# Two feature norms of a decoder step: sums of squares with tokens on partitions, deviation on three columns, result spread by TensorE

## What is computed

```python
def layer_norm(x, g=None, b=None):
    xf = x.astype(jnp.float32)
    mu = jnp.mean(xf, axis=-1, keepdims=True)
    var = jnp.mean(jnp.square(xf - mu), axis=-1, keepdims=True)
    y = (xf - mu) * lax.rsqrt(var + LN_EPS)
    if g is not None:
        y = y * g + b
    return y

def trunk_layer(x, c, pos, lw, st, mla_past):
    mod = jax.nn.silu(c) @ lw['w_ada'] + lw['b_ada']
    sh1, sc1, g1, sh2, sc2, g2 = jnp.split(mod[:, None, :], 6, axis=-1)
    u = x * (1.0 + sc1) + sh1
    mix, new_st = mixer_branches(u, pos, lw, st, mla_past)
    x = layer_norm(DEEPNORM_ALPHA * x + g1 * mix, lw['ln1_g'], lw['ln1_b'])
    u2 = x * (1.0 + sc2) + sh2
    f = (jax.nn.silu(u2 @ lw['w1']) * (u2 @ lw['w3'])) @ lw['w2']
    x = layer_norm(DEEPNORM_ALPHA * x + g2 * f, lw['ln2_g'], lw['ln2_b'])
    return x, new_st
```

## Time and profile before

| | |
|---|---|
| median of 3 runs | 1848.11 us (1847.59 to 1851.08) |
| the profiled execution | 1859.16 us, its span 1857.5 us |
| PE busy | 1707.7 us, 92% of the span |
| weight loads (PEld, beside PE) | 1476.6 us, 79% |
| DVE, ACT, POOL busy | 817.4, 738.3, 705.9 us |
| mean granted PE clock | 0.96 |

### The profile page before, as it was taken

How to read it: one execution, slowest core, us unless ns; L and a number is a source line. 1 busy time by engine, 2 the same in 40 slices (tenths; PEclk the granted TensorE clock), 3 DMA queues, 4 the chain that set the end, 5 groups by cost and what they waited for, 6 DMA issues and landing times. The chain is left out here.

```text
span 1857.5 us, 30323 instructions
## 1 busy us (share of the span) xinstructions
PE 1707.7 (92%) x10994; PEld 1476.6 (79%) x10994; DVE 817.4 (44%) x1881; ACT 738.3 (40%) x1112; POOL 705.9 (38%) x446
## 2 busy tenths in 40 slices
PE   3899999999999979999839999999999999899997
PEld 1788789987668869999718878898866677799996
DVE  0545367656431353332314642766654313533233
ACT  1444644333434344442224555342335342544332
POOL 0534456645123423333114444566361144233331
PEclk8899999999999989999969999999999999899999
DMA  9265424428575343444072653353475843444430
GB/s 355 90 222 189 143 93 158 159 91 278 183 282 178 134 181 141 155 151 145 23 294 91 238 201 102 109 186 133 127 270 178 283 172 126 173 142 153 155 141 29
DMA packets 73247, 309.10 MB, mean 166 GB/s; under 512 B 15555, under 2 KB 25091, under 8 KB 43011
## 3 DMA queue, kind: packets, MB, share of 16 engines
q1 hardware_dynamic: 73090, 307.09, 46.4%
HBM read 291.81 MB, written 15.25 MB: 165 GB/s over the span
## 5 line engine op out<-in xcount | busy, mean ns | idle before, releaser
L2052 POOL TENSOR_TENSOR wlx<-ring,wh 128x1024 fp32r<-128x1024 f32 x172 | 409.5, 2381 | 692.3 <-ACT wh L1069 686.2
L440 PE MATMUL zps<-uhi,wh 128*128 128x320 f32 x1232 | 386.4, 326 | 1.9 <-DVE qabs L1538 1.7
L441 PE MATMUL zps<-ulo,wh 128*128 128x320 f32 x1232 | 371.9, 314 | 0.0
L1069 ACT ACTIVATE wh<-ring 128x1024 fp32r<-128x1024 f32 x172 | 182.2, 1060 | 366.1 <-PE zps L441 229.9
L2157 POOL TENSOR_TENSOR wlo<-ring,whi 128x1024 fp32r<-128x1024 f32 x66 | 160.3, 2429 | 310.6 <-ACT whi L1069 310.3
L440 PEld LDWEIGHTS zps<-uhi,wh 128*128 128x128 f32 x1232 | 237.9, 193 | 15.8 <-issue 7.7
L441 PEld LDWEIGHTS zps<-ulo,wh 128*128 128x128 f32 x1232 | 238.2, 193 | 1.2 <-issue 0.4
L913 PE MATMUL zps<-xhi,whi 128*128 128x320 f32 x688 | 213.8, 311 | 0.0
L914 PE MATMUL zps<-xlo,whi 128*128 128x320 f32 x688 | 213.3, 310 | 0.0
L915 PE MATMUL zps<-xhi,wlo 128*128 128x320 f32 x688 | 213.2, 310 | 0.0
L445 PE MATMUL zps<-uhi,wlx 128*128 128x320 f32 x1232 | 207.8, 311 | 0.0
(11 more groups left out here) (285 smaller groups left out, 2570.6 us busy)
## 6 DMA issues: line engine op xcount, KB each, us to landing
ring<-wpack_dram SPq DMA_DIRECT2D x222, 1024.0 KB, 4.9
arena<-cache_dram SPq DMA_DIRECT2D x128, 320.0 KB, 4.8
arena<-stateA_dram SPq DMA_DIRECT2D x2, 2064.0 KB, 9.5
o_cn_s<-arena SPq DMA_DIRECT2D x2, 2064.0 KB, 11.2
arena<-stateD_dram SPq DMA_DIRECT2D x2, 2048.0 KB, 11.6
o_ret_s<-arena SPq DMA_DIRECT2D x2, 2048.0 KB, 11.0
x<-o_y SPq DMA_DIRECT2D x2, 1280.0 KB, 7.5
o_y<-x SPq DMA_DIRECT2D x4, 640.0 KB, 3.0
```

The lines of the kernel that those rows point to most:

```text
L440: nc.tensor.matmul(o, hi[:, k * P:(k + 1) * P], xh[:, k, :], start=k == 0, stop=False)
L441: last = nc.tensor.matmul(o, hi[:, k * P:(k + 1) * P], xl[:, k, :], start=False, stop=False)
L1069: return nc.scalar.activation(out, in_, func, **kw).then_inc(*ev(sem, label))
L2052: G().tensor_tensor(wlx[:, n % RING, half], ring[:, n % RING, half], wh[:, i, :], ALU.subtract).then_inc(*ev("pool_l", (q, i)))
```

## The change

It alters how the two norms get from the squares to the reciprocal deviation; the mean, the centring, the squares and the scaling stay.

- Sums of squares: the squares become the stationary operand, 128 tokens at a time (tokens 0 to 127, 128 to 255, 192 to 319), and one column of ones the moving one. That is three matmuls for each of the 8 feature blocks, each with one column of output. The sums lie in three columns, with tokens on partitions.
- The square root and the reciprocal work on these three columns, in `stats[:, 16:19]`, in place of 320 columns.
- A new step brings the reciprocals back to all partitions: for each group of tokens PE takes the column, broadcast to 128 columns, as stationary operand and columns of the identity as moving one, which writes the token's value in every partition. The result lies in a bank of its own, named `rstd`, which DVE's scaling reads. PE waits for the reciprocal before it, and DVE for PE after it.
- In norm 1 block 22 with its transposes stays between the sums of squares and the new step; block 23 comes after the new step.

```diff
@@ -261,6 +261,7 @@
         stats = sb("stats", [P, 128])
+        rsd = stats[:, 16:19]
@@ -879,13 +880,21 @@
-                        ps = bank("m", ("var", which), ("dve_r", ("xn", which, KC - 1)))
+                        ps = bank("m", ("var", which), ("act_n", ("std", which)))
                         for k in range(KC):
                             pe.wait_ge(*at("act_n", ("sq", which, k)))
-                            last = nc.tensor.matmul(ps[:, 0:T], ones, acc[:, k, :], start=k == 0, stop=k == KC - 1)
+                            for t, t0 in enumerate((0, P, T - P)):
+                                last = nc.tensor.matmul(ps[:, t:t + 1], acc[:, k, t0:t0 + P], ones[:, 0:1], start=k == 0 and t == 0, stop=k == KC - 1 and t == 2)
                         last.then_inc(*ev("pe_m", ("var", which)))
                         if which == 1:
-                            ada(22, 24, through=False)
+                            ada(22, 23, through=False)
+                        pe.wait_ge(*at("dve_r", ("rs", which)))
+                        ps = bank("m", ("rstd", which), ("dve_r", ("xn", which, KC - 1)))
+                        for t, (t0, tn) in enumerate(TOK):
+                            last = nc.tensor.matmul(ps[:, t0:t0 + tn], rsd[:, t:t + 1].to_broadcast([P, P]), ident[:, P - tn:P], start=True, stop=True)
+                        last.then_inc(*ev("pe_m", ("rstd", which)))
+                        if which == 1:
+                            ada(23, 24, through=False)
@@ -1389,7 +1398,7 @@
-                        go("act_n", ("std", which), std[:], m(("var", which))[:, 0:T], ACT.Sqrt, bias=cs("eps")[:, 0:1], scale=1.0 / D_MODEL)
+                        go("act_n", ("std", which), rsd, m(("var", which))[:, 0:3], ACT.Sqrt, bias=cs("eps")[:, 0:1], scale=1.0 / D_MODEL)
@@ -1978,9 +1987,8 @@
                         dve.wait_ge(*at("act_n", ("std", which)))
-                        V().reciprocal(banks["var", which][:, 0:T], std[:]).then_inc(*ev("dve_r", ("rs", which)))
-                        dve.wait_ge(*at("dve_r", ("rs", which)))
-                        return banks["var", which][:, 0:T]
+                        V().reciprocal(rsd, rsd).then_inc(*ev("dve_r", ("rs", which)))
+                        return m(("rstd", which))[:, 0:T]
```

## The result

The changed kernel takes 1866.3 us (median of 4 runs, 1862.8 to 1875.39) for 1848.11 before: ratio 1.0103, 95% interval 1.0064 to 1.0142, so it is slower by 12 to 26 us. The forecast was 1865.3.

A forecast was written before the change was run, and what follows sets the result against it. TensorE, busy 92%, bounds the kernel, with nothing hidden in the norms' serial chain. At the lower clock +3.3 us in each norm 2 and +5.3 in each norm 1 sum to +17.2 on 1848.11: 1865.3, range 1850 to 1871.

The forecast's parts named there:

- The sweep at full clock: Sums of squares on PE in each norm: 48 passes at 0.116 us plus tail, 5.64 us, +1.10 a norm.
- lower bound of 0.05 us a pass: Sums of squares: least time of a pass, read from 16 loads of 32 columns in 0.80 us.
- Rival 2: Sums of squares: one-column passes take less than 0.116 us, perhaps 0.068; sum -9.6 us, 1838.5; chance 0.05.
- The fall: PE's clock halves during each norm's sums of squares, lengthening them: sweep end +3.3 us in norm 1, +3.6 in norm 2.
- a later start of the scaling moves everything behind it by as much: Norm 1 into the first FFN tile: DVE sets the tile's end, so L2010 later by x moves everything behind by x.
- Sqrt and reciprocal: Each norm, on 3 columns: Sqrt 0.30 for 0.54 us, -0.24; reciprocal 0.16 to 0.17 for 2.17, -2.00.
- The spread: New PE step before the scaling: six passes 0.96 us, 1.0 with handoffs; 1.9 with them at the lower clock.
- Block 22 and transposes uncovered: Norm 1: PE's wait for the reciprocal stands behind them, 1.60 us at full clock, about 2.95 at the lower.
- Rival 1: The clock holds through all sweeps because PE's loads count as work; +1.5 us, 1849.6, up to 1852; chance 0.19.
- Rival 3: Norm 1, lower clock: ACT's late L1415 decides, up to +1 us per norm 1, 1867; chance within the forecast's 0.74.

The follow-up runs named there:

- cols128: Changed kernel with 128 columns of ones streamed in each pass of the sums of squares in place of one; ratio to the kernel before 1.0000.
- cols64: Changed kernel with 64 columns of ones streamed in each pass of the sums of squares in place of one; ratio to the kernel before 1.0065.
- warm128: Changed kernel with 128 columns a pass and four unused wide matmuls on PE ahead of the sums of squares; ratio to the kernel before 0.9997.
- ordwarm: Changed kernel with 128 columns a pass, spread before block 22, ACT's block 22/23 copies behind its FFN input, four unused matmuls before the sweep; ratio to before 0.9998.
- warm1: Changed kernel, still one column a pass, with four unused wide matmuls on PE ahead of the sums of squares; ratio to the kernel before 1.0025.
- short2: Kernel before with only the reciprocal cut to 3 columns, scaling by the deviation, so its results are other numbers; ratio to the kernel before 0.9939.

## Why the prediction was right

The time (1865.3 for 1866.3) and its cause, the clock falling in the sweeps, hold. That the time came out within 1 us is luck: two errors in the sum had opposite signs, the four runs lie between 1862.8 and 1875.4, and the moment of the fall differs from one execution to the next.

- **The sweep at full clock, 5.64 us.** Measured 5.54 to 5.63 where the clock held (cols128, cols64, warm128, ordwarm). The lower bound of 0.05 us a pass, from loads of 32 columns, was never near. Rival 2 is out. Its own sum was off besides: 48 passes of 0.068 take 3.3 us and not 2.8, so it stood for about -8 us and not -9.6.
- **The fall.** That it comes in each norm was right, and a pass at half clock was 10.17 / 48 = 0.212 us for 0.213. Its moment in norm 1 was the mis-sized term: I bounded it 2.0 to 4.9 us into the sweep, it came 0.5 and 0.2 us in. I had it come 3.0 us at the earliest after PE went quiet ahead of the sweep; it came 1.4 and 1.2 us after that. warm1 shows that the gap counts; whether the narrow blocks ahead of it do was not tested by itself. In norm 2 (1.5 and 3.0 us in, for 1.8 to 4.9) one of two lay within the bounds. Sweep's start to scaling was +6.7 and +6.8 in norm 1 for my +5.3, +3.8 and +2.5 in norm 2 for my +3.3: 19.8 for 17.2.
- **Given back, unforeseen.** Behind the scaling of norm 1, 1.7 us (layer 0) and 0.3 (layer 1) came back: in layer 0, with another history of the clock, PE's second FFN tile ran at 1.00, where before it ran at 0.50 until 683.1. So my reading that a later start of the scaling moves everything behind it by as much held in layer 1 only. Net 18.0.
- **Sqrt and reciprocal**, -0.24 and -2.00: measured -0.27 and -1.98 in the chain, and short2 shows that all of the latter lies on the path.
- **The spread**: 0.78 to 0.88 us at full clock and 1.54 at half for my 0.96 and 1.8, handoffs left out.
- **Block 22 and transposes uncovered**: 2.70 us between sweep and spread for 2.95, and 1.42 for 1.60 at full clock (cols128). Moving them gains 1.75 a norm at half clock and 0.76 at full, since the wait for the reciprocal takes their place.
- **Rival 1, the clock holds, 1849.6.** cols128 is that case but for one sweep: +0.5 in norm 1 and -0.26 in norm 2 to the scaling, so +0.5 in all for my +1.5, and a ratio of 1.000. So, within the interval of the ratio (0.3% either way), the clock is all of the loss.
- **Rival 3, ACT's queue.** Its first L1424 started 1.40 us after the scaling did, for 0.52 before, yet PE still waited for DVE: 0.78 us in layer 0 and 1.02 in layer 1 ahead of the sixth L936 (before, 1.01 ahead of the fifth L927). So it cost nothing, as the forecast had it.

The sweep of the changed kernel had no gap in it and lost its clock in all four norms. The Trainium skill (TensorE: Matmul & The Clock Gate, "Why this matters for your kernels") says that drops are avoided by leaving no long idle gap between bursts; the traces don't agree for narrow passes. And a gap of only 1 us, ahead of the sweep, counted: with it filled the fall came 3.8 us into the sweep for 0.5 (norm 1, layer 0) and 3.1 for 1.5 (norm 2).

## What to carry to other kernels

Replacing wide matmuls by many loads with one streamed column can cost the clock: look in the trace at what such runs, and the gap ahead of them, did to the granted clock, and stream columns behind each load that cost no time (128 were free here). On a path where nothing hides, count passes and not columns, and let an idle engine add operands beforehand: 12 passes fewer in each norm gave 5.0 us here in four sweeps. Work moved from a serial path to beside an engine that is the bound there isn't free.

## What the hardware showed unexpectedly

- A matmul pass with a fresh 128x128 load started 0.11 us after the one before it (0.116 with its share of the run's tail) whether 1, 64 or 128 fp32 columns followed, with the clock at 1.00, and 0.21 us after it at 0.50.
- With 128 columns a pass the clock, fallen at the sweep's start, came back 3.4 us later inside it, in three of three cases, as it did once with 320 columns; with one column it stayed at 0.50 to the end of all twelve sweeps (up to 10.3 us).
- With about 1 us of waiting ahead of a one-column run the fall came 0.1 to 1.5 us into it in six of eight, and 3.0 and 3.1 in two; without, 3.1 to 3.8 in four of four.
